# Half of the query latents moved into the first tile of the second attention, in a one-core Trainium2 kernel

## What is computed

```python
c = rms_norm(c_kv, kv_g)
q_lat = jnp.einsum('bshd,hcd->bshc', qh, w_uk).astype(jnp.float32) * (ATT_HEAD_DIM ** -0.5)
# for each block of 128 queries: the keys kept are the 256 with the highest index score
s = jnp.einsum('bthc,btkc->bthk', ql_b, c_sel)
p = jax.nn.softmax(s, axis=-1)
o_lat = jnp.einsum('bthk,btkc->bthc', p, c_sel)
out = jnp.einsum('bshc,hcd->bshd', o_lat.astype(w_uv.dtype), w_uv)
```

## Time and profile before

| what | value |
|---|---|
| median of 3 runs | 2439.09 us (2437.64 to 2439.29) |
| profiled execution, own time | 2439.81 us |
| its span in the trace | 2438.0 us |
| PE busy | 2336.4 us (96%) |
| DVE busy | 1343.5 us (55%) |
| ACT busy | 943.1 us (39%) |
| POOL busy | 417.0 us (17%) |
| chain that ended last | PE 84%, DVE 10%, ACT 3%, issue 2% |

### The profile page before, as it was taken

The page is one execution under the profiler, slowest core; times in us unless marked ns, Lnnn a source line. Parts: engine busy times, 40 slices in busy tenths (PEclk is TensorE's granted clock), DMA queues, the critical chain, the costliest instruction groups (busy, mean ns, idle before and its releaser), DMA issues.

```text
span 2438.0 us, 32455 instructions
## 1 busy us (share of the span) xinstructions
PE 2336.4 (96%) x12937; PEld 1777.6 (73%) x12937; DVE 1343.5 (55%) x2298; ACT 943.1 (39%) x1689; POOL 417.0 (17%) x614
## 2 busy tenths in 40 slices
PE   7999999999999999999999999999899789799998
PEld 7887888888777898788888887778665354545554
DVE  5567876332233366577844222247667767945444
ACT  5335555231114244455633111232444748432231
POOL 0034320000000001332100000000548552501011
PEclk9999999999999999999999999999999999899999
DMA  6010001122213220100022221143101011110000
GB/s 217 31 53 1 1 1 52 46 52 52 52 46 118 86 86 18 35 2 1 1 70 53 52 52 27 60 143 109 35 1 45 10 46 65 38 52 26 26 18 35
DMA packets 106646, 116.93 MB, mean 48 GB/s; under 512 B 20832, under 2 KB 78912, under 8 KB 106496
## 3 DMA queue, kind: packets, MB, share of 16 engines
q1 hardware_dynamic: 106208, 113.81, 14.9%
q10 hardware_dynamic: 288, 1.05, 0.1%
HBM read 96.82 MB, written 16.84 MB: 47 GB/s over the span
## 4 chain that ended last, share of the span: by engine, by line
PE 84%; DVE 10%; ACT 3%; issue 2%; DMA 0%; POOL 0%; SPq 0%; DVEq 0%; ACTq 0%
PE PS L731 7%; PE PS L791 7%; PE PS L794 7%; PE PS L797 7%; PE PS L563 6%; PE PS L755 5%; PE PS L1203 4%; PE PS L1172 2%; PE PS L844 2%; PE PS L1150 2%; PE PS L949 2%; PE PS L841 2%; PE PS L840 2%; PE PS L837 2%; DVE R2a L2514 2%
## 5 line engine op out<-in xcount | busy, mean ns | idle before, releaser
L794 PE MATMUL PS<-hLo,R2bR 128*128 128x512 f32 x768 | 298.9, 389 | 0.0
L791 PE MATMUL PS<-hHi,R2bR 128*128 128x512 f32 x752 | 293.2, 390 | 0.0
L797 PE MATMUL PS<-hHi,R2bR 128*128 128x512 f32 x752 | 292.6, 389 | 0.0
L2283 DVE TENSOR_TENSOR R2bR<-W,R2bR 128x1024 fp32r<-128x1024 f32 x48 | 57.5, 1222 | 267.3 <-ACT R2bR L1574 267.3
L1641 ACT ACTIVATE R3a<-PS,pT 128x512 f32<-128x512 f32 x64 | 42.3, 688 | 403.6 <-PE PS L797 403.5
L949 PE MATMUL PS<-hT,W 128*128 128x512 f32 x384 | 166.1, 593 | 0.7 <-ACT R L1737 0.7
L794 PEld LDWEIGHTS PS<-hLo,R2bR 128*128 128x128 f32 x768 | 144.3, 188 | 30.0
L1590 ACT ACTIVATE R2b<-PS,negm 128x1024 f32<-128x1024 f32 x128 | 142.6, 1114 | 59.9 <-DVE negm L2262 59.7
L2262 DVE TENSOR_REDUCE negm<-PS 128x1 f32<-128x1024 f32 x128 | 156.3, 1221 | 14.8 <-PE PS L731 14.1
L791 PEld LDWEIGHTS PS<-hHi,R2bR 128*128 128x128 f32 x752 | 141.3, 188 | 30.1 <-issue 0.6
L797 PEld LDWEIGHTS PS<-hHi,R2bR 128*128 128x128 f32 x752 | 141.3, 188 | 29.0
(11 more groups left out here) (494 smaller groups left out, 5355.0 us busy)
## 6 DMA issues: line engine op xcount, KB each, us to landing
W<-in_w_in SPq DMA_DIRECT2D x10, 2048.0 KB, 8.2
W<-in_w_in SPq DMA_DIRECT2D x33, 512.0 KB, 4.3
W<-in_w_out SPq DMA_DIRECT2D x6, 2048.0 KB, 7.7
xres<-R SPq DMA_DIRECT2D x2, 4096.0 KB, 15.3
R<-xres SPq DMA_DIRECT2D x2, 4096.0 KB, 18.3
W<-in_w_in SPq DMA_DIRECT2D x4, 1024.0 KB, 6.5
R3a<-rsums SPq DMA_DIRECT2D x16, 256.0 KB, 5.3
W<-in_w_attn_proj SPq DMA_DIRECT2D x16, 256.0 KB, 5.8
```

The costliest lines, as they stand in the source:

```text
L791: mm = pe.matmul(o, wHi[c % 2][:, k, :], hi, start=(k == 0), stop=False)
L794: mm = pe.matmul(o, wHi[c % 2][:, k, :], hLo[:, k, ns], start=False, stop=False)
L797: mm = pe.matmul(o, wLo[c % 2][:, k, :], hi, start=False, stop=(k == 7))
L2283: dve.tensor_tensor(wLo[c % 2], w, wHi[c % 2].bitcast(F32), ALU.subtract).then_inc(s_wlo, 1)
```

## The change

Before the attention, only half 0 of the latents is made, product h in bank (1 + h) mod 8: all eight banks once. ACT copies those of the even heads, DVE those of the odd heads. Half 1 of head h is made inside tile 0: PE issues it in unit u = h between the scores of unit u + 1 and the transposes of unit u, in bank 5 (even heads) or 7 (odd heads); DVE copies it in unit u after the copy of the transposed probabilities of unit u - 1. SP's loads of gain, bias and residual wait for the last of these products instead.

```diff
@@ TensorE
             ql_free = {}
+            def query_latents(h, n, b):
+                o = begin(b)
+                ql_free[h, n] = (b, bk.count(b))
+                r_ = slice(VD * (h % 2), VD * (h % 2) + VD)
+                pe.matmul(o, wukT[r_, h // 2, :], qT2[r_, h // 2, n * 512:(n + 1) * 512],
+                          start=True, stop=True).then_inc(full[b], 1)
+
             for h in range(H):
-                for n in range(2):
-                    b = (1 + 2 * h + n) % 8
-                    o = begin(b)
-                    ql_free[h, n] = (b, bk.count(b))
-                    marks["ql", h, n] = bk.count(b)
-                    r_ = slice(VD * (h % 2), VD * (h % 2) + VD)
-                    pe.matmul(o, wukT[r_, h // 2, :], qT2[r_, h // 2, n * 512:(n + 1) * 512],
-                              start=True, stop=True).then_inc(full[b], 1)
-            marks["qlat"] = bk.count(0)
+                query_latents(h, 0, (1 + h) % 8)
...
                 if u + 1 < H * NT:
                     scores2(u + 1)
 
+                if t == 0:
+                    query_latents(h, 1, 5 + 2 * (h % 2))
+                if u == 7:
+                    marks["qlat"] = bk.count(7)
@@ SyncE
-            sp.wait_ge(full[0], marks["qlat"])
+            sp.wait_ge(full[7], marks["qlat"])
@@ ScalarE
             for h in range(H):
-                for n in range(2):
-                    b = (1 + 2 * h + n) % 8
-                    if n == 1:
-                        bk.take(b)
-                        continue
+                b = (1 + h) % 8
+                if h % 2 == 0:
                     o = arrive(b)
                     act.activation(qlT[:, h, 0:512], o, ACT.Copy, scale=64.0 ** -0.5).then_inc(free[b], 1)
+                else:
+                    bk.take(b)
...
                 b = 2 * (u % 2)
                 bk.take(b)
+                if t == 0:
+                    bk.take(5 + 2 * (h % 2))
@@ VectorE
-            for h in range(H):
-                b = (2 + 2 * h) % 8
-                dve.wait_ge(full[b], marks["ql", h, 1])
-                dve.tensor_scalar(qlT[:, h, 512:1024], PS[:, b, :], 64.0 ** -0.5, None, ALU.mult
+            for h in range(1, H, 2):
+                b = (1 + h) % 8
+                dve.wait_ge(full[b], marks["attention"][b])
+                dve.tensor_scalar(qlT[:, h, 0:512], PS[:, b, :], 64.0 ** -0.5, None, ALU.mult
                                   ).then_inc(free[b], 1)
...
                 if u >= 1:
                     turned(u - 1)
+                if t == 0:
+                    o = arrive(5 + 2 * (h % 2))
+                    dve.tensor_scalar(qlT[:, h, 512:1024], o, 64.0 ** -0.5, None, ALU.mult
+                                      ).then_inc(free[5 + 2 * (h % 2)], 1)
```

## The result

The changed kernel takes 2453.06 us (median of 4, 2451.97 to 2453.97) against 2439.19 (median of 4, 2437.64 to 2439.81): ratio 1.0058, 95% interval 1.004 to 1.0075. It is 13.9 us **slower**; the forecast was no change at 2440.5 with a range to 2443.2. The profiled execution took 2452.36 us, its span is 2450.5.

What follows compares the result with a forecast made beforehand. PE was taken as the bound, busy nearly all the time, with waits at the seam before attention. First minimum 4.38 us earlier, tile 0 5.83 longer: +1.45 on 2439.81, less 0.72, gives 2440.5 us; range 2436.8 to 2443.2.

Steps and rivals of the forecast that it cites:

- The front: From the end of DVE's search to the first scores: four DVE copies remain, scores start 4.57 us earlier, at 2131.90.
- the hidden loads of SP: Gain, bias and residual loads, issued at about 2146, end near 2155, before the first residual at 2163.47: no cost.
- ACT's copies: Before the attention, ACT's copies fall from eight to four; no cost or gain, since ACT waited for PE there.
- the part on tile 0: First minimum of tile 0 to that of tile 1: 14.2 us against 8.38, so 5.83 us more.
- The loop: Tile 0 at the full clock: two units take 3.02 us, 1.51 a unit, six units 9.06 us.
- The slower rival: Clock stays low through tile 0, PE bounds each unit at 2.5 us: 2448.2 us in all; chance 0.08.
- The rival on switches: Half-array to whole-array switches in tile 0 add 0.29 us a unit, 2.3 us on top: 2442.8 us; chance 0.15.

Runs made afterwards that it cites:

- the run without pairs: Kernel before the change, heads reordered 0, 2, 4, 6, 1, 3, 5, 7 so neighbouring products share one half of the array: 2444.73 us in one execution.
- the run with whole-array products: Changed kernel, with the eight products inside tile 0 using all 128 rows of the array in place of 64: 2440.95 us in one execution.

## Why the prediction was wrong

- **The front** was right: 4.56 us earlier, forecast 4.57. So were the hidden loads of SP, ACT's copies, and the place of the cost, between the end of the search and the first projection.
- **The step that failed** is in the part on tile 0: "I take the 1.2 GHz level at 2131.90 and its end 3.8 us after PE resumes, as before". The 3.8 us were read from pairs of products and carried over to lone ones. I had priced that the pairs were lost in PE's time (0.86 us each and not half of that), but not that they were lost for the clock. At 1.2 GHz the units stayed at 2.86 us or more to the end of the tile, where I had two at 2.3 (4.65 / 2) and six at 1.51. That lone products don't lift the clock is what the run without pairs shows in its place (0.50 for over 20 us), and the run with whole-array products shows the rise at the forecast time once the rows are all in use.
- **The size.** From the first minimum of tile 0 (2131.44) to that of tile 1 (2156.57) it is 25.1 us; forecast 14.2. The other 1.4 us lie in tile 1, where the clock was low until about 2161. The first minimum came 0.91 us after the scores and not 0.61, 0.3 later. With the 4.6 us gained in front: 25.1 - 8.4 + 1.4 + 0.3 - 4.6 give the 13.9 but for rounding. Of it about 8 x 0.5 = 4 us are the switches at the low clock, an estimate from the chains of the changed kernel and of the whole-array run.
- **The loop** at the full clock was right for a tile without switches: 1.48 us a unit in the whole-array run, against 1.51, bound by DVE and ACT as I had it. In the tile as it is, with the clock up, it is 1.57, but there PE's own work with its switches binds, which I had at 1.25 (0.12 + 0.27 + 0.86), so the closeness of 1.57 to 1.51 is in part luck. The stretches from the first copy to the first projection were 1.0 and 0.85 us longer than before, against a forecast of 1.45. With the clock up, the change is what I said it was, as far as one execution each can tell: nothing.
- **The slower rival** named the outcome and the place, with its price too low (2.5 us a unit against 2.86, most of it the switches it left out; 2448.2 against 2453.06), and it had 0.08. Its reason was that the dense run ahead of the attention is gone, not that a lone product uses half of the array. What spoke against it in my text, "PE would be busy almost without a gap at that clock", was true and did not help: PE was busy 25.97 of 26.00 us. Reading the same rows more closely would have shown that the two stretches ahead of a rise held pairs in one case and a latent output over the whole array in the other; no row showed the clock rising after lone half-array work, so its chance was far too small.
- **The rival on switches** had a price near the mark, 0.29 us a unit against about 0.4 of PE's time at the full clock, but not its effect: it put the price on top of the loop, and most of it hid beside the loop (0.8 us for the tile in place of 2.3). At the low clock, where PE binds, 0.5 us a unit showed in full. The Trainium skill, "TensorEngine Tiling (Array Packing)", section Key Properties, has a change of mode drain TensorE; these times agree with it, though the pure drain was not measured by itself.
- **The Trainium skill**, "TensorE: Matmul & The Clock Gate", Part 1, says that the clock is set by how busy PE has been. The runs here differ from the plain reading of that: at a busy share of practically 1 the clock stayed at 0.50 for 26 us, and for over 20 us in the run without pairs; lone products or pairs made the difference there.

## What to carry to other kernels

Before matmuls that use half of TensorE's rows are moved, look at what runs beside them: neighbours in the other half share their time, and they also count for the clock. Put alone between whole-array matmuls, such a product also brings two switches, whose cost hides only where another engine binds. A step placed behind a long wait of TensorE starts at the low clock, and work that keeps a high clock up may not be enough to bring it back, so price such a step at both levels, and ask of every rise in the trace what work went ahead of it. And where an engine that comes late has copies to make, first look for an engine that is idle at that time; here that was worth 7.6 us, with no work moved at all.

## What the runs showed of the hardware

The busy share of TensorE alone does not tell the clock it is granted: 25.97 us of 26.00 with lone 64-row products at 0.50, and 8.06 us of 10.90 with pairs at 0.99. The level at which a stretch begins counts too: the same tile 0 ran at 1.00 throughout when it began there, and at 0.50 throughout when it began low. Two switches between half-array and whole-array matmuls took about 0.4 us of PE's time at the full clock (1.57 against 1.19 us a unit) and 0.5 at the low one (2.86 against 2.35). I had expected neither of the first two. How much of the array has to work, and for how long, these runs leave open.
